# Carries kept in SBUF between two stages, both scan directions summed on chip, and the stage's products in another order

## The reference

```python
def step(state, inp):
    r_t, w_t, k_t, v_t, a_t, b_t = inp
    sa = jnp.einsum('dbhij,dbhj->dbhi', state, a_t)
    state = (state * w_t[..., None, :] + sa[..., :, None] * b_t[..., None, :]
             + v_t[..., :, None] * k_t[..., None, :])
    y_t = jnp.einsum('dbhij,dbhj->dbhi', state, r_t)
    return state, y_t

state0 = jnp.zeros((2, B, H, N, N), f32)
_, ys = lax.scan(step, state0, xs)
y = jnp.moveaxis(ys[:, 0] + ys[::-1, 1], 0, 1)   # the two directions are summed
...
bonus = jnp.sum(r * k * r_k, axis=-1, keepdims=True) * v
return (y + bonus).reshape(B, S, RW_WIDTH)
```

## Time and profile before

| | |
|---|---|
| median of 3 runs | 3979.37 us (3975.54 to 3981.8) |
| profiled execution | 3975.73 us, of which the span of the profile is 3974.0 |
| TensorE busy in the span | 3594.7 us (90%) |
| DVE / ACT / POOL busy | 2378.0 / 1426.8 / 436.5 us |
| unit stage, TensorE busy in 830 us | 790.21 us |
| chain stage, TensorE busy in 176 us | 73.64 us |

### The profile page before, as it was taken

One profiled execution on the slowest core, in us unless ns is written; L12 is line 12 of the kernel. 1 busy time (PEld: TensorE's weight loads), 2 busy tenths in 40 slices (PEclk: granted clock), 3 DMA queues, 4 the chain that ended last, 5 costly groups with the idle time before them and its releaser, 6 DMA issues. The chain is left out here.

```text
span 3974.0 us, 60663 instructions
## 1 busy us (share of the span) xinstructions
PE 3594.7 (90%) x21081; PEld 2386.5 (60%) x21081; DVE 2378.0 (60%) x4080; ACT 1426.8 (36%) x2571; POOL 436.5 (11%) x702
## 2 busy tenths in 40 slices
PE   7999996899999949999999944699999968999999
PEld 6778775344444427888888744367767744444444
DVE  3567655799999935555555522577777753444443
ACT  3444443132333212222222200466666642323232
POOL 0243334000000001121122100000000000000000
PEclk9999998999999969999999977799999988999999
DMA  4343434512313224434434467310000023222221
GB/s 141 129 162 111 135 117 133 189 56 107 127 63 109 82 80 127 131 124 127 132 125 128 129 195 242 108 40 13 11 13 13 13 94 120 83 83 83 83 83 44
DMA packets 347850, 406.15 MB, mean 102 GB/s; under 512 B 123980, under 2 KB 261912, under 8 KB 345312
## 3 DMA queue, kind: packets, MB, share of 16 engines
q1 hardware_dynamic: 341984, 394.26, 30.0%
q10 hardware_dynamic: 5760, 10.49, 0.7%
HBM read 221.17 MB, written 183.50 MB: 102 GB/s over the span
## 5 line engine op out<-in xcount | busy, mean ns | idle before, releaser
L906 PE MATMUL rs_tm<-rs_w,rs_uT 128*128 128x512 f32 x1600 | 692.1, 594 | 25.5 <-DMA rs_w<-in_w_in_dram 25.5
L906 PEld LDWEIGHTS rs_tm<-rs_w,rs_uT 128*128 128x128 f32 x1600 | 303.2, 191 | 400.7 <-issue 398.7
L561 PE MATMUL cv_pj<-cv_uT,cv_w 128*128 128x257 f32 (+1 forms) x2240 | 502.9, 382 | 0.8 <-DVEq L420 0.8
L561 PEld LDWEIGHTS cv_pj<-cv_uT,cv_w 128*128 128x128 f32 (+1 forms) x2240 | 410.1, 186 | 90.0 <-issue 22.9
L1540 PE MATMUL at_g<-at_kT,at_qz 64*128 64x512 f32 x1088 | 301.9, 632 | 28.5 <-DMA at_kT<-scratch_q_kT 23.8
L834 DVE TENSOR_TENSOR rs_tmp<-rs_tt,rs_al 128x63 f32<-128x63 f32 (+31 forms) x315 | 284.1, 902 | 23.6 <-DMA rs_al<-scratch_ablk 14.2
L836 DVE TENSOR_TENSOR rs_tt<-rs_tt,rs_tmp 128x63 f32<-128x63 f32 (+31 forms) x315 | 288.9, 917 | 10.8
L1563 PEld LDWEIGHTS at_pb<-at_v,at_attT 128*128 128x128 f32 x2176 | 250.6, 193 | 64.7 <-issue 47.0
L1823 PE MATMUL fn_hb<-fn_wo,fn_mixT 128*128 128x512 f32 x640 | 279.7, 595 | 0.3 <-ACT fn_mixT L1683 0.3
L1823 PE MATMUL fn_gb<-fn_wg,fn_hT 128*128 128x512 f32 x640 | 278.0, 592 | 1.7 <-ACT fn_hT L1683 1.7
L1563 PE MATMUL at_pb<-at_v,at_attT 128*128 128x128 f32 x2176 | 266.1, 280 | 13.0 <-ACT at_attT L1450 13.0
(11 more groups left out here) (236 smaller groups left out, 5632.2 us busy)
## 6 DMA issues: line engine op xcount, KB each, us to landing
un_pk<-scratch_packs SPq DMA_DIRECT2D x80, 640.0 KB, 3.9
scratch_packs<-cv_pk SPq DMA_DIRECT2D x20, 2048.0 KB, 6.7
scratch_carry<-un_carry_out SPq DMA_DIRECT2D x80, 256.0 KB, 2.0
ch_cb<-scratch_carry SPq DMA_DIRECT2D x40, 512.0 KB, 8.2
scratch_local<-un_local_out SPq DMA_DIRECT2D x80, 192.0 KB, 1.9
cv_x<-in_x_dram SPq DMA_DIRECT2D x20, 512.0 KB, 3.4
scratch_uT<-cv_uT SPq DMA_DIRECT2D x5, 2048.0 KB, 7.9
scratch_ablk<-cv_ab SPq DMA_DIRECT2D x80, 128.0 KB, 2.3
```

The source lines that it names most:

```text
L561: last = nc.tensor.matmul(pj[n % 3][0:r, 0:HALF], w[:, c, m * P:m * P + r], uT[b % 2][:, c, HALF * hf:HALF * hf + HALF], start=(c == 0), s ...
L906: last = nc.tensor.matmul(tm[n % 4][:, :], uT[b % 2][:, k, half], w[:, k, 512 * u:512 * u + 512], start=(k == 0), stop=(k == KC - 1))
```

## The change

Of the 80 units, the carries of the 20 of group 0 still go to memory (`carry` has 20 entries). Those of the other 60 are written straight into a new SBUF tensor `kept`, which lives through units and chain. A unit adds its two directions: ACT copies direction 0 into `local_out`, DVE adds direction 1 from PSUM. `outputs` runs the narrow products of both directions first, the two head halves alternating, then the wide ones, and the first half is released before the last pair of products. The loops of units and chain become straight code.

The chain loads only group 0's carries, by SP. ACT issues the loads of all 20 chunks' local outputs at once into `ysum`, which stays in SBUF; DVE adds both directions' outputs into it, and when a chunk has had both (the last half of the steps of its sequence) ACT stores it, once. The output stage loads one y instead of two, and POOL's addition is gone.

```diff
-            with eng.Fori(0, NI // 2 - 1) as j:
-                body(j * 2, j, 0, True)
-                body(j * 2 + 1, j, 1, True)
-            body(NI - 2, NI // 2 - 1, 0, True)
-            body(NI - 1, NI // 2 - 1, 1, False)
+            for n in range(NI):
+                body(n, n // 2, n % 2, n + 1 < NI)
+
+        def carry_at(n, par, rows, d, first, last):
+            if n < NCH:
+                return carry_out[par][rows, d, first:last]
+            return kept[rows, n - NCH, d, first:last]
...
-                sp.wait_ge(s["y_evac"], n * 4 + 8)
-                sp.dma_start(carry[n], carry_out[par][:, :, :]).then_inc(s[f"carry{par}"], 16)
+                sp.wait_ge(s["own_evac"], n * 2 + 4)
+                if n < NCH:
+                    sp.dma_start(carry[n], carry_out[par][:, :, :]).then_inc(s[f"carry{par}"], 16)
                 sp.wait_ge(s["bonus_evac"], n * 2 + 4)
+                sp.wait_ge(s["sum_evac"], n * 2 + 4)
                 sp.dma_start(local[n], local_out[par][:, :, :]).then_inc(s[f"local{par}"], 16)
...
-                    nc.scalar.copy(local_out[par][ys, 0:2, :], ob[h][ys, 0:384].rearrange("p (d t) -> p d t", d=2)[:, :, 0:P]).then_inc(s["y_evac"], 1)
+                    nc.scalar.copy(local_out[par][ys, 0, :], ob[h][ys, 0:P]).then_inc(s["y_evac"], 1)
                     act.wait_ge(s["carry_evac"], n * 4 + 2 * h + 10)
-                    nc.scalar.copy(carry_out[par][hs, :, 192:256], ob[h][hs, 384:512].rearrange("p (d c) -> p d c", d=2)).then_inc(s["y_evac"], 1)
+                    nc.scalar.copy(carry_at(n, par, hs, slice(0, 2), 192, 256), ob[h][hs, 384:512].rearrange("p (d c) -> p d c", d=2)).then_inc(s["own_evac"], 1)
...
-                    hs = slice(64 * h, 64 * h + 64)
+                    hs, ys = slice(64 * h, 64 * h + 64), slice(64 - 64 * h, 128 - 64 * h)
                     for d in range(2):
-                        nc.vector.scalar_tensor_tensor(carry_out[par][hs, d, 0:192], ob[h][hs, 192 * d:192 * d + 192], fp[par][hs, d:d + 1], ad[par][hs, d, :],
+                        nc.vector.scalar_tensor_tensor(carry_at(n, par, hs, d, 0, 192), ob[h][hs, 192 * d:192 * d + 192], fp[par][hs, d:d + 1], ad[par][hs, d, :],
                                                        ALU.mult, ALU.add).then_inc(s["carry_evac"], 1)
+                    dve.wait_ge(s["y_evac"], n * 2 + h + 1)
+                    nc.vector.tensor_tensor(local_out[par][ys, 0, :], ob[h][ys, 192:192 + P], local_out[par][ys, 0, :], ALU.add).then_inc(s["sum_evac"], 1)
...
-                pe.wait_ge(s["y_evac"], n * 4 + 4)
-                for h in range(2):
-                    hs, ys = slice(64 * h, 64 * h + 64), slice(64 - 64 * h, 128 - 64 * h)
-                    V = vz[par][:, 64 + 64 * h:128 + 64 * h]
-                    for d in range(2):
-                        B, K, = bk_tok[par][:, 0, d, hs], bk_tok[par][:, 1, d, hs]
-                        W, Z = wz[par][:, d, h, hs], wz[par][:, d, h, ys]
-                        mm(ob[h][hs, 384 + 64 * d:448 + 64 * d], B, Z, start=True, stop=False)
-                        mm(ob[h][hs, 384 + 64 * d:448 + 64 * d], K, V, start=False, stop=True)
-                        mm(ob[h][hs, 192 * d + P:192 * d + 192], W, B, start=True, stop=True)
-                    for d in range(2):
+                pe.wait_ge(s["own_evac"], n * 2 + 2)
+                pe.wait_ge(s["sum_evac"], n * 2 + 2)
+                own = [slice(64 * h, 64 * h + 64) for h in range(2)]
+                V = [vz[par][:, 64 + 64 * h:128 + 64 * h] for h in range(2)]
+                for d in range(2):
+                    at = 384 + 64 * d
+                    for h in range(2):
+                        mm(ob[h][own[h], at:at + 64], bk_tok[par][:, 0, d, own[h]], wz[par][:, d, h, own[1 - h]], start=True, stop=False)
+                    for h in range(2):
+                        mm(ob[h][own[h], at:at + 64], bk_tok[par][:, 1, d, own[h]], V[h], start=False, stop=True)
+                    for h in range(2):
+                        mm(ob[h][own[h], 192 * d + P:192 * d + 192], wz[par][:, d, h, own[h]], bk_tok[par][:, 0, d, own[h]], start=True, stop=True)
+                for d in range(2):
+                    for h in range(2):
                         o = ob[h][:, 192 * d:192 * d + P]
                         mm(o, wz[par][:, d, h, :], su[par][:, d, h, SU_RB[d]:SU_RB[d] + P], start=True, stop=False)
                         last = mm(o, vz[par][:, P * h:P * h + P], su[par][:, d, h, SU_RK[d]:SU_RK[d] + P], start=False, stop=True)
-                    last.then_inc(s["out_ready"], 1)
+                        if d:
+                            last.then_inc(s["out_ready"], 1)
...
-        cb = [ph.sb(f"cb{i}", [P, 2, G, 256]) for i in range(2)]
-        lb = [ph.sb(f"lb{i}", [P, 2, G, P]) for i in range(2)]
-        yo = [ph.sb(f"yo{i}", [P, 2, G, P]) for i in range(2)]
+        cb = [ph.sb(f"cb{i}", [P, 2, 256]) for i in range(2)]
+        ysum = ph.sb("ysum", [P, NCH, G * P])
...
+        steps = [(i, first, t, (t, 2 * first + count - 1 - t), t - first >= count // 2)
+                 for i, (first, count) in enumerate(sequences) for t in range(first, first + count)]
+
+        def carry_at(t, chunk, rows, d, g, a, b):
+            if g == 0:
+                return cb[t % 2][rows, d, a:b]
+            return kept[rows, (g - 1) * NCH + chunk[d], d, a:b]
 
         @block.sync
         def _(sp):
-            def body(t, chunk, par, half, i):
-                sp.wait_ge(s["y_evac"], t * 2 + 1)
+            for i, first, t, chunk, last in steps:
+                if t >= 2:
+                    sp.wait_ge(s["y_evac"], 2 * t - 2)
                 for d in range(2):
-                    sp.dma_start(cb[par][:, d, :, :], carry_v[chunk[d]][d]).then_inc(s[f"loaded{par}"], 16)
-                    sp.dma_start(lb[par][:, d, :, :], local_v[chunk[d]][d]).then_inc(s[f"loaded{par}"], 16)
-            steps(sp, body)
+                    sp.dma_start(cb[t % 2][:, d, :], carry_v[chunk[d]][d]).then_inc(s[f"carry{t % 2}"], 16)
 
         @block.scalar
         def _(act):
-            def body(t, chunk, par, half, i):
-                act.wait_ge(s["y_evac"], t * 2 + 5)
-                for d in range(2):
-                    act.dma_start(y[d][chunk[d]], yo[par][:, d, :, :].rearrange("p g c -> p (g c)")).then_inc(s[f"stored{par}"], 16)
-            steps(act, body)
-            for par in range(2):
-                act.wait_ge(s[f"stored{par}"], NCH * 16 + 32)
+            for i, first, t, chunk, last in steps:
+                if not last:
+                    for c in chunk:
+                        act.dma_start(ysum[:, c, :].rearrange("p (g t) -> p g t", t=P), local_v[c][0]).then_inc(loaded[c], 16)
+            for i, first, t, chunk, last in steps:
+                if last:
+                    act.wait_ge(s["y_evac"], 2 * t + 2)
+                    for c in chunk:
+                        act.dma_start(y[c], ysum[:, c, :]).then_inc(s["stored"], 16)
+            act.wait_ge(s["stored"], 16 * NCH)
...
-                nc.vector.tensor_tensor(H[1 - par][:, :, :], hb[par][:, :].rearrange("p (u c) -> p u c", c=64),
-                                        cb[par][:, :, :, 192:256].rearrange("p d g c -> p (d g) c"), ALU.add).then_inc(s["h_evac"], 1)
-                dve.wait_ge(s["stored%d" % par], half * 32 + 32)
+                new, update = H[1 - t % 2], hb[t % 2][:, :].rearrange("p (u c) -> p u c", c=64)
+                nc.vector.tensor_tensor(new[:, ::G, :], update[:, ::G, :], cb[t % 2][:, :, 192:256], ALU.add)
+                for d in range(2):
+                    ins = nc.vector.tensor_tensor(new[:, G * d + 1:G * d + G, :], update[:, G * d + 1:G * d + G, :],
+                                                  kept[:, chunk[d]::NCH, d, 192:256], ALU.add)
+                ins.then_inc(s["h_evac"], 1)
                 dve.wait_ge(s["y_ready"], t + 1)
+                if last:
+                    dve.wait_ge(s["y_evac"], 2 * t)
                 for d in range(2):
-                    nc.vector.tensor_tensor(yo[par][:, d, :, :], yb[2 * par + d][:, :].rearrange("p (g t) -> p g t", t=P),
-                                            lb[par][:, d, :, :], ALU.add).then_inc(s["y_evac"], 1)
-            steps(dve, body, start)
+                    c = chunk[d]
+                    dve.wait_ge(loaded[c], 16)
+                    nc.vector.tensor_tensor(ysum[:, c, :], yb[2 * (t % 2) + d][:, :], ysum[:, c, :], ALU.add).then_inc(s["y_evac"], 1)
...
+                pe.wait_ge(s[f"carry{t % 2}"], 32 * (t // 2) + 32)
                 pe.wait_ge(s["h_evac"], t + i + 1)
+                old = H[t % 2]
                 units = [(d, g, h) for d in range(2) for g in range(G) for h in range(2)]
                 for d, g, h in units:
+                    hs, u = slice(64 * h, 64 * h + 64), G * d + g
```

(24 more changed lines are left out.)

108 lines of the change are left out of this document (36 added, 72 removed).

## The result

The changed kernel takes 3911.2 us (median of four runs, 3906.6 to 3914.4), the kernel before beside it 3980.5 (3975.5 to 3981.8). The ratio is 0.983, with a 95% interval of 0.981 to 0.984: faster by 69 us. The forecast was 3884 us with a range of 3842 to 3906, so the sign is right, the saving is 27 us short, and the time lies 5 us above the range.

What follows compares the result with a forecast made beforehand. Transfers were taken to bound the chain, two equally long loops (TensorE's and SP's, 10.24 us) the unit stage. 3975.73 - 83 (chain) - 11 (units) - 1 (output) = 3880.7 profiled; the median, 3.6 above, gives 3884 us, range 3842 to 3906.

Steps and rivals of the forecast that it cites:

- Chain: Chain stage: transfers bound it; with fewer loads and stores it takes 93 us instead of 176, 83 us saved.
- the rival of slow carries: Chain: among preloads and stores the carries still land in 8.2 us, stage 141 us, total 3932 us; chance 0.07.
- 0.45 a step: Chain: added to 3.65 us a step because preloads and stores share the DMA engines with the carries, giving 4.1.
- Unit stage: 80 units: each takes 10.1 us for 10.24, 11 us saved, with ends of 0 and 45.
- SP's: 4.59 + 0.37 + 0.1 + 2.59 + 2.46: Unit stage, SP's loop: scores to L1187's end, late masks, address arithmetic, load issues, landing; 10.11 us a unit.
- the overlap rival: Unit stage: column halves overlap, TensorE's loop falls to 9.45, SP's 9.74 decides, 40 us saved, total 3855; chance 0.41.
- the slower rival: Unit stage: fetching straight code stalls TensorE 2 us once a unit, 160 us, total 4044 us; chance 0.03.
- (c): Unit stage, outputs: narrow products alternate column halves; taken as 0 a unit, -0.67 us if weight loads overlap.
- (b): Unit stage, outputs: new order drops one way into the wide shape and one out; -0.35 us, of 0 to -0.38.
- (d): Unit stage: DVE's two additions of the directions make the masks late, delaying the second scores; +0.37 us a unit.
- (a): Unit stage, straight code: TensorE's scores to L1201 6.16 for 6.30, SP's issues 2.59 for 2.98, address arithmetic 0.1 us.
- Output: Output stage: POOL's addition goes and 256 KB less are loaded ahead of the bias row; 1 us saved.

Runs made afterwards that it cites:

- e10: Changed kernel with TensorE's unit code alone back in a loop, all other engines straight: 3871.8 us, ratio 0.9736.
- e3: Changed kernel with its unit stage back in loops on all engines, the last two units straight: 3893.6 us, ratio 0.9782.
- e6: e3 with SP's unit code alone straight, the other engines in loops: 3868.1 us, ratio 0.9728.
- e14: e10 with one further load of 32 KB per unit into a buffer that nothing reads: 3885.8 us, ratio 0.9768.
- the pairs of kernels: Two pairs differing only in whether TensorE's unit code is straight or looped: unit stage differs by 45.6 and 41.7 us.
- e4: Changed kernel with three buffers instead of two for a unit's loads, issued one unit earlier: 3826.1 us, ratio 0.9612.
- e7: Kernel before with its unit stage in straight code and three buffers for a unit's loads: 3954.9 us, ratio 0.9945.
- e12: e7 with the products of outputs in the new order: 3875.6 us, ratio 0.9742.
- e8: e4 with VectorE's two local sums moved behind the next unit's first masks: 3800.9 us, ratio 0.956.
- e2: Kernel before, in its loops, with the 20 products of outputs in the new order: 3977.8 us, ratio 0.9993.

## Why the prediction was wrong, point by point

**Chain: right.** 83 forecast, 82.7 measured. The carries land in 2.6 us as assumed in the median of 40, and TensorE's wait for them is 33.6 us in all where it was 101.6 for the local outputs before. The DMA issues of the changed kernel in this stage (KB each, us to landing):

```profile
ch_cb<-scratch_carry SPq DMA_DIRECT2D x40, 128.0 KB, 2.6
ch_ysum<-scratch_local ACTq DMA_DIRECT2D x20, 256.0 KB, 6.3
```

No addition waits for the preloads at 6.3 us, but the carries beside them are slow. From first to last the carries' landing spreads like this:

```profile
DMA to landing us min/median/max: 2.0/2.6/5.9
```

The slow ones are those of the first six steps, issued while the preloads run: the second carry of a step lands in 3.8 to 5.9 us, and TensorE waits 4.9 and 3.8 us before its third and fifth steps. In steps 9 to 14 they land in 2.0 to 2.7. So the rival of slow carries was half true for the first steps and wrong for the rest. The steps, from one update of the state to the next, are 2.8 to 7.8 us long and 4.19 in the mean, where the sum had 4.1: its 0.45 a step for shared DMA engines was about right as a mean, though it falls on few steps. The clock is 0.84 in the mean and not 1; the sum had no term for that, and the 0.45 covered it as well. That the total came out within a microsecond is in part luck.

**Unit stage: wrong, in the step "SP's: 4.59 + 0.37 + 0.1 + 2.59 + 2.46".** The first three were fair: e10 shows 4.70 without a late mask, against 4.59 + 0.1. The issues are shorter than forecast, 2.31 for 2.59. The landing is the term that failed: 2.46 forecast, 3.28 measured. That turned 10.1 us a unit into 10.51, and 11 us saved into 20 lost. It failed twice.

First, 2.46 was read from one unit and carried over as if it were a latency that begins with the last issue. It isn't. That unit's products are straight code, but its loads were still issued in SP's loop, from 2281.25 to 2284.23:

```profile
2281.25 0.35 SPq L968 DMA_DIRECT2D un_pk<-scratch_packs  x1
```

From its first issue to the scores it is 5.44, and the sum put the 2.46 behind issues of 2.59, 5.05 in all. The time from the *first* issue is what stays nearly the same: 5.33 in the kernel before (2.93 + 2.40), 5.34 in e3, 5.27 in e6 and e10, and even 5.43 with a sixth issue (e14). What SP gains by issuing faster, the last load gives back by landing 2.96 after its issue. An undisturbed loop of SP's is 4.70 + 5.27 = 9.97, and not 9.74 as the overlap rival had it.

Second, TensorE's straight code fetches its instructions in the same stretch, and the scores come 3.28 after the last issue in the mean. Late loads leave TensorE idle, now and then its clock drops (ten stretches at the half clock from 1540 us on, 48 us in all; none in e10), and the first leg grows from 4.70 to 4.90 in the mean. Together 0.54 a unit, 43 us of the stage, and the pairs of kernels say 42 and 46. The forecast had no term for fetching. I had priced it in the slower rival alone, as a stall of TensorE, 2 us once a unit, with a chance of 0.03; the fetching came (62 for 80 units), but it strikes a transfer with no slack, not the engine that fetches. The evidence I took against it was a conv stage that fetches without a wait. TensorE never waited for a load in those 700 us, so they say nothing on a stage in which the next load is always just in time. By the Trainium skill ("Runtime: NRT & Kernel Launch", Instruction fetch mechanics) a block's crossing is mostly hidden; for TensorE itself the runs agree (e4), for the loads beside it they don't.

**(c) column halves: wrong.** I took 0; the rows show 0.03 us for each narrow record, and e7 against e12 gives 78.5 us for the whole order, 0.97 a unit, against 0.35 + 0.67 = 1.02 for (b) and (c) at its other end. The Trainium skill ("TensorE: Matmul & The Clock Gate", Part 3) says that weight loads overlap running products only when the row group differs. By that the term would be 0. This trace doesn't bear out the "only": these products share all 128 rows, and two of different column halves start 0.007 us apart. The forecast of what TensorE's loop would be with it, 9.45, is 9.42 in e4.

**(d) the sums: right in size, hidden in place.** 0.37 forecast, 0.31 by e4 and e8 (9.42 and 9.11). In the changed kernel TensorE waited for the loads anyway.

**(a) straight code: right for the engine's own pace.** TensorE's 6.16 + 3.94 = 10.10 without the later terms is 10.01 in e7. SP's part was worth 28.7 us (e3 to e6), 0.36 a unit, of which 0.30 is the earlier first issue and 0.07 what the faster issues left.

**Output:** 1 forecast, 4.9 in the two profiles. Over all kernels here, the five with the old output stage take 720.5 us in the mean (718.7 to 721.6) and the eleven with the new one 717.9 (716.7 to 718.9), so 2.6 is the better figure, and part of the 4.9 is chance.

The sum of the profiled executions is 82.7 + 1.7 + 4.9 saved and 19.7 lost. The balance of two equal loops was read rightly, and that shortening one alone gives nothing (e2). The failure was to shorten the second on paper, by a landing time that I tied to the last issue, and to leave the fetches out of it.

**Open.** That a fetch among a unit's loads makes them land some 0.9 us later is shown unit by unit. Why 16 KB delay 832 KB by so much more than their share of bytes is not; no run here shows where the two meet. What the part of the 5.27 us is that doesn't go with the bytes is open too. Nor was a version tried that keeps TensorE in its loop and has three buffers.

## What to carry to other kernels

When two engines' loops are equally long, test the edit with slack first: a third buffer made an order of products worth 78 us that had been worth nothing, and turned a saving of 69 us into 154; moving two sums then made it 175. A load's landing is to be measured from the first issue of its group; if it doesn't move with the last issue, issuing faster gains nothing. In this kernel straight code paid on the engine that issues the loads (SP), and cost most on the engine with the most instructions (TensorE), as long as the loads had no slack. When a stage fetches instructions, compare the units in which a fetch meets the loads with those in which none does: one trace is enough to see the cost.
